# Decoder layer: probability-times-v products of two blocks issued together, with a second buffer of turned probabilities

## What is computed

```python
qb = q.reshape(B, NB, BLOCK, Hkv, G, hd)            # NB = 8 blocks of 128 tokens, Hkv = 4, G = 4, hd = 64
kk = [block before | block]; vv = [block before | block]
scores = einsum('bnqhgd,bnkhd->bnhgqk', qb, kk) * hd ** -0.5      # masked to the band of 128 keys
mx = maximum(scores.max(-1), sink)
p = exp(scores - mx)
probs = p / (p.sum(-1) + exp(sink - mx))
out = einsum('bnhgqk,bnkhd->bnqhgd', probs, vv)     # the products that the change regroups
att * silu(az)                                       # then the gate and w_att_branch
```

## Time and profile before

| | |
|---|---|
| time, median of 3 runs | 1351.73 us (1351.0 to 1352.35) |
| time of the profiled execution | 1350.42 us |
| its span | 1348.7 us |
| PE busy | 1310.7 us, 97% |
| DVE busy | 654.4 us, 49% |
| ACT busy | 426.2 us, 32% |
| POOL busy | 623.7 us, 46% |
| share of PE in the chain that ended last | 89% |
| granted clock of PE, mean | 0.996 |

### The profile page before, as it was taken

The page is one execution under the profiler, slowest core; times in us unless marked ns, Lnnn a source line. Parts: engine busy times, 40 slices in busy tenths (PEclk is TensorE's granted clock), DMA queues, the critical chain, the costliest instruction groups (busy, mean ns, idle before and its releaser), DMA issues.

```text
span 1348.7 us, 20154 instructions
## 1 busy us (share of the span) xinstructions
PE 1310.7 (97%) x6941; PEld 1112.2 (82%) x6941; DVE 654.4 (49%) x1345; ACT 426.2 (32%) x1057; POOL 623.7 (46%) x836
## 2 busy tenths in 40 slices
PE   5799999999999999999999999999999999999997
PEld 3587978889778888889888988898889888788886
DVE  5676775857770000254555355435544431544335
ACT  5456565554620000133313331333232311311111
POOL 3507042160674444492576167517660555567240
PEclk9899999999999999999999999999999999999999
DMA  9702011020202220420320041004200133321602
GB/s 318 202 16 64 17 42 38 1 63 0 54 25 78 75 65 31 125 63 1 94 62 16 0 109 47 16 0 109 52 26 16 47 110 93 110 92 49 203 24 102
DMA packets 125045, 89.43 MB, mean 66 GB/s; under 512 B 12465, under 2 KB 118081, under 8 KB 124994
## 3 DMA queue, kind: packets, MB, share of 16 engines
q1 hardware_dynamic: 121312, 76.11, 20.3%
q10 hardware_dynamic: 3682, 12.66, 2.8%
HBM read 80.36 MB, written 8.41 MB: 66 GB/s over the span
## 4 chain that ended last, share of the span: by engine, by line
PE 89%; DVE 6%; ACT 2%; issue 1%; SPq 1%; DMA 1%; DVEq 0%; ACTq 0%
PE pp L579 26%; PE pp L580 26%; PE pp L581 26%; PE pp L736 2%; PE pp L843 2%; DVE y_lo L1482 1%; PE pp L719 1%; PE pp L720 1%; PE pp L727 1%; PE pp L835 1%; DVE prob_t L1433 1%; PE pp L704 1%; DMA w_mod<-w_ada 1%; SPq L396 1%; PE pp L828 1%
## 5 line engine op out<-in xcount | busy, mean ns | idle before, releaser
L513 POOL TENSOR_TENSOR w_hi<-raw,ones 128x256 fp32r<-128x256 f32 x388 | 262.5, 707 | 595.1 <-ACTq L370 326.8
L579 PE MATMUL pp<-h_hi,w_hi 128*128 128x512 f32 x896 | 350.0, 391 | 0.5 <-DVEq L1502 0.5
L580 PE MATMUL pp<-h_lo,w_hi 128*128 128x512 f32 x896 | 349.0, 390 | 0.0
L581 PE MATMUL pp<-h_hi,w_lo 128*128 128x512 f32 x896 | 348.8, 389 | 0.0
L517 POOL TENSOR_TENSOR w_lo<-raw,w_hi 128x256 fp32r<-128x256 f32 x388 | 319.7, 855 | 7.6
L579 PEld LDWEIGHTS pp<-h_hi,w_hi 128*128 128x128 f32 x896 | 168.3, 188 | 35.5 <-DVEq L1502 0.9
L581 PEld LDWEIGHTS pp<-h_hi,w_lo 128*128 128x128 f32 x896 | 168.2, 188 | 35.0
L580 PEld LDWEIGHTS pp<-h_lo,w_hi 128*128 128x128 f32 x896 | 168.3, 188 | 33.6
L579 PE MATMUL pp<-w_hi,h_hi 128*128 128x256 f32 (+2 forms) x496 | 154.7, 312 | 1.4 <-ACT v_tok L1018 1.2
L581 PE MATMUL pp<-w_hi,h_lo 128*128 128x256 f32 (+2 forms) x496 | 153.1, 309 | 0.0
L580 PE MATMUL pp<-w_lo,h_hi 128*128 128x256 f32 (+2 forms) x496 | 152.9, 308 | 0.0
(11 more groups left out here) (260 smaller groups left out, 1953.0 us busy)
## 6 DMA issues: line engine op xcount, KB each, us to landing
raw<-w_in SPq DMA_DIRECT2D x70, 512.0 KB, 4.0
w_mod<-w_ada SPq DMA_DIRECT2D x16, 512.0 KB, 9.3
x_in<-x SPq DMA_DIRECT2D x4, 1024.0 KB, 9.7
raw<-w_att SPq DMA_DIRECT2D x8, 512.0 KB, 5.5
merged_dram<-mix_a ACTq DMA_DIRECT2D x8, 512.0 KB, 2.6
w_gate<-w_ada ACTq DMA_DIRECT2D x8, 512.0 KB, 3.6
raw<-w_m SPq DMA_DIRECT2D x8, 512.0 KB, 3.8
mix_in<-merged_dram ACTq DMA_DIRECT2D x8, 512.0 KB, 3.2
```

Of the source, the lines that this page charges most:

```text
L513: ins = pool.tensor_tensor(hi[:, q, :], raw[:, s, q, :], one[:, q, :], ALU.mult)
L579: pe.matmul(o, lh, rh, start=first, stop=False)
L580: pe.matmul(o, lh, rl, start=False, stop=False)
L581: return pe.matmul(o, ll, rh, start=False, stop=last)
```

## The change

Products with v are made for two blocks (a pair p = blocks 2p and 2p+1) in one group: in rounds 6, 8 and 10, and the fourth pair in round 0 of the next head. Rounds 5, 7, 9 and 11 have none. The two blocks of a pair use two `prob_t` buffers and the two halves of the columns of bank 7. `copy_att` then copies a pair at once (512 columns), in ACT's rounds 7, 9, 11 and 13. Counts of `att_full` and `att_copied` are halved everywhere. No matmul and no DVE instruction is added or removed; ACT has four copies per head where it had eight.

```diff
-        prob_t = place("prob_t", [P, 2, 4 * P], F32, SCR + 20480)
+        prob_t = [place("prob_t", [P, 2, 4 * P], F32, SCR + 20480), place("prob_t_odd", [P, 2, 4 * P], F32, SCR)]
...
-            def weigh_v(i, m):
-                after(pe, prob_t_ready, prob_parts(i, m + 1))
-                after(pe, v_copied, NB * i + m + 1)
-                after(pe, att_copied, NB * i + m)
-                for odd in range(2):
-                    for old in range(1 if m == 0 else 0, 2):
-                        ins = pe.matmul(pp[odd * HD:(odd + 1) * HD, 7, 0:2 * P], v_tok[:, m - 1 + old, :],
-                                        prob_t[:, old, odd * 2 * P:(odd + 1) * 2 * P],
...
+            def weigh_v(i, p):
+                after(pe, prob_t_ready, prob_parts(i, 2 * p + 2))
+                after(pe, v_copied, NB * i + 2 * p + 2)
+                after(pe, att_copied, NB // 2 * i + p)
+                for m in (2 * p, 2 * p + 1):
+                    for odd in range(2):
+                        for old in range(1 if m == 0 else 0, 2):
+                            ins = pe.matmul(pp[odd * HD:(odd + 1) * HD, 7, m % 2 * 2 * P:(m % 2 + 1) * 2 * P], v_tok[:, m - 1 + old, :],
+                                            prob_t[m % 2][:, old, odd * 2 * P:(odd + 1) * 2 * P],
...
                     if u == 0 and before_head is not None:
-                        weigh_v(before_head, NB - 1)
+                        weigh_v(before_head, NB // 2 - 1)
...
-                    if 5 <= u:
-                        weigh_v(i, u - 5)
+                    if u in (6, 8, 10):
+                        weigh_v(i, u // 2 - 3)
...
-            def copy_att(i, m):
-                after(act, att_full, NB * i + m + 1)
-                dst = y[:, bass.ds(2 * i, 2), m * P:(m + 1) * P]
-                act.activation(dst, bank(7)[:, 0:2 * P].rearrange("p (a t) -> p a t", a=2), ACT.Copy).then_inc(att_copied, 1)
+            def copy_att(i, p):
+                after(act, att_full, NB // 2 * i + p + 1)
+                dst = y[:, bass.ds(2 * i, 2), 2 * p * P:2 * (p + 1) * P].rearrange("p a (m t) -> p a m t", m=2)
+                act.activation(dst, bank(7).rearrange("p (m a t) -> p a m t", m=2, a=2), ACT.Copy).then_inc(att_copied, 1)
...
-                    if 6 <= u:
-                        copy_att(i, u - 6)
+                    if u in (7, 9, 11, 13):
+                        copy_att(i, (u - 7) // 2)
...
             def split_window(i, m):
                 after(dve, probs_turned, NB * i + m + 1)
-                after(dve, att_full, NB * i + m)
+                after(dve, att_full, NB // 2 * i + m // 2)
...
-                        dve.tensor_tensor(prob_t[:, part, :].rearrange("p (g t) -> p g t", g=4),
+                        dve.tensor_tensor(prob_t[m % 2][:, part, :].rearrange("p (g t) -> p g t", g=4),
```

More of the change, by code:

```diff
@@ L728, in turn_probs @@
                 ins.then_inc(probs_turned, 1)
-            def weigh_v(i, m):
-                after(pe, prob_t_ready, prob_parts(i, m + 1))
-                after(pe, v_copied, NB * i + m + 1)
-                after(pe, att_copied, NB * i + m)
-                for odd in range(2):
-                    for old in range(1 if m == 0 else 0, 2):
-                        ins = pe.matmul(pp[odd * HD:(odd + 1) * HD, 7, 0:2 * P], v_tok[:, m - 1 + old, :],
-                                        prob_t[:, old, odd * 2 * P:(odd + 1) * 2 * P],
-                                        start=(old == (1 if m == 0 else 0)), stop=(old == 1), skip_group_check=True)
+            def weigh_v(i, p):
[7 more added lines that the diff above has]
+                                            prob_t[m % 2][:, old, odd * 2 * P:(odd + 1) * 2 * P],
+                                            start=(old == (1 if m == 0 else 0)), stop=(old == 1), skip_group_check=True)
                 ins.then_inc(att_full, 1)
@@ L748, in gate_row_step @@
                     pe.wait_ge(row_step, 5)
-                    after(pe, att_copied, NB)
+                    after(pe, att_copied, NB // 2)
                     for q, row in enumerate((row_b, row_m)):
@@ L806, in _ @@
             pe.transpose(bank(2)[:, 0:P], row_all[:, :], ident[:, :]).then_inc(gates_turned, 1)
-            weigh_v(KVH - 1, NB - 1)
+            weigh_v(KVH - 1, NB // 2 - 1)
             with pe.Fori(0, 4, 1) as i:
@@ L1016, in copy_v @@
                 after(act, rope_product, 2 * (NB * i + m + 1))
-                after(act, att_full, NB * i)
+                after(act, att_full, NB // 2 * i)
                 act.activation(v_tok[:, m, :], bank(b)[:, 5 * HD:6 * HD], ACT.Copy).then_inc(v_copied, 1)
@@ L1463, in gate_head @@
                     after(dve, bank_free[b], n + 1)
-                after(dve, att_copied, NB * (i + 1))
+                after(dve, att_copied, NB // 2 * (i + 1))
                 for half in range(2):
```

## The result

The changed kernel takes 1359.71 us (median of 4 runs, 1359.16 to 1359.85) beside 1351.45 for the kernel before: ratio 1.006, 95% interval 1.0049 to 1.0072, 8.3 us more. Run again later beside another set, it gave 1359.60 against 1351.20, ratio 1.006. The forecast was 1358.5, 6.8 us over its own base.

The account below looks back on a forecast made before the run. PE was taken as the bound, each attention round set by whichever of PE or the probabilities arrives last. Four heads +7.4, +6.4 after the last head's gain, copies +0.44: +6.8 us on 1351.73, forecast 1358.5; range 1354.0 to 1361.5.

Parts of the forecast that it names:

- The ring, and which side arrives last: Attention rounds: PE's scores, then DVE and ACT's probabilities; PE arrives last in later rounds, probabilities in round 4 (PE waits 0.29 us).
- Even rounds pay in full: Rounds 6, 8, 10 and next head's 0: PE arrives last, so added products cost +0.44, then +0.88 us each.
- The fixed part of a group, 0.24 us: Each group of products on PE: entering and leaving the 64-column form; 16 fewer groups would save 3.8 us without waits.
- Round 9, "Gain 0.30": Round 9 loses a group; from line 1425's end to the second load of `prob`'s transposes, only 0.30 us can be gained.
- Round 10, +0.88: Round 10 gets four more products at 0.22 us each, PE arriving last: 0.88 us longer.
- Round 11, "Gain 0": Round 11 loses 1.02 us of work, but the next head's first unit waits for round 10's Silu; gain 0, except last head.
- The copies, 0.44: ACT's 512-column copies, exposed before head 2 and behind the last head: +0.22 us each, 0.44 taken from 0 to 0.44.
- 0.22 for each product: PE's cost per product in a group, beside the fixed part: groups of four take 1.12 us, of two 0.68.
- the rival without a difference: Products of two blocks overlap better in one group, an added one costing 0.11 us: 1352.3 us, 6% chance.
- The rival of POOL's splits: POOL's splits fall on worse DVE instructions in rounds 9 to 11, 0.7 us per head: +2.8, 1361.3 us, 12% chance.
- The faster rival: Probabilities don't hold PE in odd rounds, so the fixed part's saving stands: -3.8 +0.44, 1348.4 us, 5% chance.

## Why the prediction was right

Direction and range held: 1359.7 lies in 1354.0 to 1361.5, and the loss was 8.3 us where 6.8 were forecast. The mechanism held too, in rounds 5 to 8 and 0 nearly to the number; in rounds 9 to 11 the sum is nearer than its terms, by luck. Step by step:

- **The ring, and which side arrives last.** Right. Rounds 5 and 7 gave 0.34 and 0.45 of the 0.68 and 1.12 us of work that left them. The run with them empty and the one with them refilled show it from both sides.
- **Even rounds pay in full.** Right for 6, 8 and 0: 0.52, 0.90 and 0.92 for 0.44, 0.88 and 0.88. Repeating the products alone cost 12.9 us, forecast 12.3.
- **The fixed part of a group, 0.24 us.** Measured 0.3.
- **Round 9, "Gain 0.30".** Wrong in size: 0.01. The sum took the time that DVE and ACT need from the scores to the probabilities as fixed (6.46 us); the longer round 8 moved DVE's chain against POOL's splits and it became 6.82. Emptied without that shift, in the run with rounds 5, 7, 9 and 11 emptied, round 9 did give 0.35. The prediction had priced such a shift at up to 0.7 us either way and left it out of the sum.
- **Round 10, +0.88.** Mis-sized for the same reason: +1.23, since the unit of round 10 now starts on the Silu of round 8's unit. Of this unit's bank the prediction said that 0.29 us was open; the slower chain, 8.35 us instead of 7.87 from the end of round 8's scores to the end of the Silu in head 2, used it up. The weight load that was held, and the one behind round 11:

```profile
282.45 0.19 PEld L579 LDWEIGHTS pp<-h_hi,w_hi 128*128 128x128 f32 x1 [0.24 <-ACT silu_az L1068]
...
298.49 0.19 PEld L579 LDWEIGHTS pp<-w_hi,h_hi 128*128 128x128 f32 x1 [1.18 <-ACT silu_az L1068]
```

- **Round 11, "Gain 0".** Right in mechanism: the first unit of the next head starts 0.05 us behind the Silu behind heads 1 and 2 in both kernels (behind head 0 it is 0.12 and 0.11), and the wait of about 1 us that was forecast is 1.16, 0.74 and 1.18. Wrong in size: 0.53 was gained, because the way to the Silu fell from 7.27 to 6.80 us in head 2. In the kernel before, POOL's split ran until 287.03 and DVE's second small instruction beside it took 0.66 us; in the changed one the split ended at 293.54 and the same instruction took 0.16:

```profile
286.38 0.66 DVE L1381 TENSOR_TENSOR sink_d<-neg_m,h_neg_sink 128x4 f32<-128x4 f32 x1
...
293.59 0.16 DVE L1382 TENSOR_TENSOR sink_d<-neg_m,h_neg_sink 128x4 f32<-128x4 f32 x1
```

- **The copies, 0.44.** Right: 0.25 before head 2, and 0.20 behind the last head until it is lost from sight in phase C.
- **"0.22 for each product."** The sum held, the reading did not: it is 0.44 for a pair of products, one for each half of the partitions (last section). That also bears on the rival without a difference: products do run side by side, but they did so before the change too.

One omission made the largest errors: the time that DVE needs was read from rows and kept, though it depends on when POOL runs beside it. Over four heads round 9 was off by +1.1 us, round 10 by +1.4 and round 11 by -1.8, and these cancel to 0.7. That the total came so near is partly luck. The rest is small and mostly one way: rounds 5 to 8 together +1.0. Phase B starts 8.6 us later, counted from the first head's round 3, where about 6 was forecast. The rival of POOL's splits ("slower still", 12%) had the cause and the direction, not the size: it left out that round 11 gains. The faster rival, which had the fixed part alone, fell: the wait for line 727 was there in every round that it would have had to be free of it.

## What to carry to other kernels

Take work out of a round in which it covers another engine's time, and you gain only what the next-late wait leaves open (here 0.34 and 0.45 us of 0.68 and 1.12); put it into a round in which the bound engine arrives last, and you pay all of it. So price each round by the slack of its next-late wait, not by the engine's busy share. Merge small groups only where the emptied round has slack for the whole group (here one of seven). Before trusting such a slack, look at what else runs beside the engine that sets it, since a round longer by 0.9 us changed the slack itself by 0.4 us or more. The one pair that did pay, once POOL's split was held back, gained 1.5 us, 0.1% of the time.

## What the runs showed that I had not expected

The products of the two halves of the partitions run side by side. With one of block 0's two products left, PE's timeline of round 5, head 2, is

```profile
242.28 0.27 PE L697 MATMUL pp<-ident,roped 128*128 128x128 f32 x1
242.49 0.65 PE L736 MATMUL pp<-prob_t,v_tok 128*64 128x256 f32 x2
243.06 0.44 PE L704 MATMUL pp<-ident,roped 128*128 128x128 f32 x2
```

The first product's start to line 704 is 0.57 us with one product, where the earlier trace rows has 0.58 for two, and in the trace of the kernel before the records of the two halves start 0.01 us apart, each pair 0.22 to 0.27 behind the one ahead. So "0.22 for each product" was half of 0.44 for a pair, one per half, and a group of a single half saves nothing; the sums held because every group had both. The Trainium skill says that different tiles can work in parallel (TensorEngine Tiling (Array Packing), Key Properties); the rows agree.

In the run with emptied rounds, 2.8 us in which PE started nothing were followed by 3.2 us at a mean granted clock of 0.52. I had expected the stretch alone to be the price.
